# Twelve one-column sums issued between the matmuls of a gate product

## What is computed

```python
def mla_branch(c_q, c_kv, k_rope, q_norm, kv_norm, w_uq, w_ukv, cos, sin):
    q = (rms_norm(c_q, q_norm) @ w_uq).reshape(bsz, seq, A_HEADS, A_NOPE + A_ROPE)
    kv = (rms_norm(c_kv, kv_norm) @ w_ukv).reshape(bsz, seq, A_HEADS, A_NOPE + A_V)
    k_rope = apply_rope(k_rope, cos, sin)
    ...
for layer in range(DEPTH):
    u = rms_norm(h, norm_pre[layer])
    proj = u @ w_in[layer]
    ...
    y_a = mla_branch(a_cq, a_ckv, a_kr, ...) * jax.nn.silu(a_g)
    ...
    y = jnp.concatenate([y_a, y_b, y_c, y_d], axis=-1) @ w_out[layer]
    h = h + rms_norm(y, norm_post[layer])
```

## Time and profile before

| | |
|---|---|
| time, median of 3 runs | 740.94 us (738.87 to 741.82) |
| the profiled execution | 739.99 us, its span 738.1 us |
| busy share of the span | PE 92%, VectorE 59%, ScalarE 45%, GpSimd 33% |
| mean granted clock of TensorE | 0.97 |
| sums of squares, layer 0 / layer 1 | 4.78 / 3.96 us on PE |

### The profile page before, as it was taken

How to read it: one execution, slowest core, us unless ns; L and a number is a source line. 1 busy time by engine, 2 the same in 40 slices (tenths; PEclk the granted TensorE clock), 3 DMA queues, 4 the chain that set the end, 5 groups by cost and what they waited for, 6 DMA issues and landing times. The chain is left out here.

```text
span 738.1 us, 10470 instructions
## 1 busy us (share of the span) xinstructions
PE 677.0 (92%) x3836; PEld 545.8 (74%) x3836; DVE 437.5 (59%) x1067; ACT 328.5 (45%) x750; POOL 242.3 (33%) x208
## 2 busy tenths in 40 slices
PE   3996999999999999789998999999999999978996
PEld 3885977888796674448997888778788777444896
DVE  4211597889886754661182148888978955566114
ACT  4422544656241634771434344456533344577121
POOL 1352352354254631000434344425323544210030
PEclk9998999999999977999999999999999998899999
DMA  8367874423122210303253387742322221030202
GB/s 266 96 221 227 261 221 117 130 72 117 57 72 72 72 57 1 114 1 112 84 143 122 119 257 229 193 128 88 101 72 72 72 73 58 0 115 1 73 29 101
DMA packets 66754, 81.48 MB, mean 110 GB/s; under 512 B 10720, under 2 KB 52320, under 8 KB 66703
## 3 DMA queue, kind: packets, MB, share of 16 engines
q1 hardware_dynamic: 66703, 80.81, 35.5%
HBM read 70.28 MB, written 13.93 MB: 114 GB/s over the span
## 5 line engine op out<-in xcount | busy, mean ns | idle before, releaser
L697 POOL TENSOR_TENSOR w_low<-w_raw,w_high 128x512 fp32r<-128x512 f32 (+2 forms) x156 | 199.9, 1314 | 397.3 <-ACT w_high L737 397.3
L1219 PE MATMUL bank<-uT,w_high 128*128 128x512 f32 x400 | 160.0, 400 | 0.0
L1221 PE MATMUL bank<-uT,w_low 128*128 128x512 f32 x400 | 158.2, 396 | 0.0
L1220 PE MATMUL bank<-uT,w_high 128*128 128x512 f32 x400 | 157.9, 395 | 0.0
L841 ACT ACTIVATE probs<-probs,negmax 128x128 f32<-128x128 f32 (+3 forms) x160 | 88.8, 558 | 89.9 <-DVE negmax L1074 89.6
L1219 PEld LDWEIGHTS bank<-uT,w_high 128*128 128x128 f32 x400 | 75.5, 189 | 18.3 <-issue 1.6
L1221 PEld LDWEIGHTS bank<-uT,w_low 128*128 128x128 f32 x400 | 75.3, 188 | 17.8
L1220 PEld LDWEIGHTS bank<-uT,w_high 128*128 128x128 f32 x400 | 75.6, 189 | 16.3
L737 ACT ACTIVATE w_high<-w_raw 128x2048 fp32r<-128x2048 f32 (+2 forms) x40 | 74.7, 1867 | 28.7 <-DMA w_raw<-in_w_out 23.8
L1219 PE MATMUL bank<-w_high,mix 128*128 128x256 f32 x256 | 72.4, 283 | 1.0 <-DVE mix L1159 1.0
L1221 PE MATMUL bank<-w_high,mix 128*128 128x256 f32 x256 | 71.6, 280 | 0.0
(11 more groups left out here) (145 smaller groups left out, 1091.4 us busy)
## 6 DMA issues: line engine op xcount, KB each, us to landing
w_raw<-in_w_in SPq DMA_DIRECT2D x28, 1024.0 KB, 5.4
w_raw<-in_w_out SPq DMA_DIRECT2D x8, 1024.0 KB, 4.9
parts_dram<-staging SPq DMA_DIRECT2D x12, 512.0 KB, 4.9
strips<-strips_dram SPq DMA_DIRECT2D x24, 256.0 KB, 4.2
dqk<-parts_dram SPq DMA_DIRECT2D x24, 256.0 KB, 4.2
hX<-in_x SPq DMA_DIRECT2D x8, 512.0 KB, 6.0
strips_dram<-table_dram SPq DMA_DIRECT2D x1, 3328.0 KB
qidx<-parts_dram SPq DMA_DIRECT2D x12, 256.0 KB, 4.2
```

Of the source, the lines that this page charges most:

```text
L697: ins = nc.gpsimd.tensor_tensor(w_low[:, s, ks, 0:w], w_raw[:, s, ks, 0:w], w_high[:, s, ks, 0:w].bitcast(F32), ALU.subtract)
L1219: nc.tensor.matmul(out_ap, lh, rh, start=start, stop=False)
L1220: nc.tensor.matmul(out_ap, lh, rl, start=False, stop=False)
L1221: return nc.tensor.matmul(out_ap, ll, rh, start=False, stop=stop)
```

## The change

The twelve sums are no longer a block of their own. `aup_head` moves ahead of the gate product `("unit", "ga", 1)`, and on PE it now only waits for the squares and takes the bank. The product's loop over its eight chunks puts, in each of the first four, one sum behind each of its three matmuls; the last sum counts up `unit_ready`. The transposes of the rotary key and VectorE's work on them become a step of their own, `krturn`, right behind the product. VectorE's folding and means stay with `aup_head` and so come ahead of the gate's evacuation. The units are numbered anew (sums, gate, rotary key in place of gate, sums, rotary key), and one VectorE copy falls away.

```diff
-SQUARES_AT, AUP_HEAD_AT = 8, 9
+SQUARES_AT = 8
+SQUARES_IN = ("unit", "ga", 1)
@@ layer_steps
         for e in ex[:half]:
-            st += [e] + topk(r[1])
+            st += [("aup_head",), e, ("krturn",)] if e == SQUARES_IN else [e] + topk(r[1])
...
-        st += {SQUARES_AT: [("squares_a",)], AUP_HEAD_AT: [("aup_head",)]}.get(j, [])
+        st += [("squares_a",)] if j == SQUARES_AT else []
@@ units_of
-    if k == "aup_head":
-        return ["dve", "dve"]
+    if k in ("aup_head", "krturn"):
+        return ["dve"]
@@ vector
                     nc.vector.tensor_copy(coef[:, 0, 0:1], s8[:, 0:1]).then_inc(emptied_by["dve"], 1)
-                    dve.wait_ge(unit_ready, n + 2)
-                    after(nc.vector.tensor_copy(krx[:], bank[:, unit_bank(n + 1), 0:NB * A_ROPE].rearrange(
-                        "p (t r) -> p t r", t=NB)))
+                if kind == "krturn":
+                    n = l * NU + UNIT_AT[step]
+                    dve.wait_ge(unit_ready, n + 1)
+                    nc.vector.tensor_copy(krx[:], bank[:, unit_bank(n), 0:NB * A_ROPE].rearrange(
+                        "p (t r) -> p t r", t=NB)).then_inc(emptied_by["dve"], 1)
+                    wait_unit_emptied(dve, n)
                     hr = A_ROPE // 2
...
-                    nc.vector.tensor_copy(coef[:, 0, 0:1], krx[:, 0, 0:1]).then_inc(emptied_by["dve"], 1)
@@ tensor
+                        elif step == SQUARES_IN:
+                            cs = slice(c * P, (c + 1) * P)
+                            sb, ts = squares_bank, slice(k * P, (k + 1) * P)
+                            nc.tensor.matmul(b, w_high[:, s, k, cs], uT[:, 0, k, :], start=k == 0, stop=False)
+                            if k < NB:
+                                nc.tensor.matmul(sb[:, k:k + 1], sq[:, 0, ts], ones[:], start=True, stop=False)
+                            nc.tensor.matmul(b, w_high[:, s, k, cs], uT[:, 1, k, :], start=False, stop=False)
+                            if k < NB:
+                                nc.tensor.matmul(sb[:, k:k + 1], sq[0:64, 1, ts], ones[0:64, :], start=False, stop=True)
+                            ins = nc.tensor.matmul(b, w_low[:, s, k, cs], uT[:, 0, k, :], start=False, stop=k == KC - 1)
+                            if k < NB:
+                                last_square = nc.tensor.matmul(sb[:, 4 + k:5 + k], sq[:, 2, ts], ones[:],
+                                                               start=True, stop=True)
+                            if k == NB - 1:
+                                last_square.then_inc(unit_ready, 1)
...
                 if kind == "aup_head":
-                    n = l * NU + UNIT_AT[step]
                     pe.wait_ge(lat_squared, l + 1)
-                    b = work_bank(n)
-                    for tb in range(NB):
-                        ts = slice(tb * P, (tb + 1) * P)
-                        nc.tensor.matmul(b[:, tb:tb + 1], sq[:, 0, ts], ones[:], start=True, stop=False)
-                        nc.tensor.matmul(b[:, tb:tb + 1], sq[0:64, 1, ts], ones[0:64, :], start=False, stop=True)
-                        ins = nc.tensor.matmul(b[:, 4 + tb:5 + tb], sq[:, 2, ts], ones[:], start=True, stop=True)
-                    ins.then_inc(unit_ready, 1)
-                    b = work_bank(n + 1)
+                    squares_bank = work_bank(l * NU + UNIT_AT[step])
+                if kind == "krturn":
+                    b = work_bank(l * NU + UNIT_AT[step])
```

## The result

The changed kernel takes 747.04 us (739.82 to 753.11, 15 executions) against 740.96 us (736.69 to 749.04) for the kernel before in the same comparison: ratio 1.0063, 95% interval 1.0037 to 1.0089. That is slower by 0.6%, and outside the predicted range. By the medians the change costs between 3.7 and 6.1 us, where 0.4 us less was predicted. A ratio leaves out, of every kernel, executions over 1.5% above its fastest (slow ones), while medians and times at half clock are over all its executions.

The account below looks back on a forecast made before the run. TensorE, at half clock after the one-column sums, bounds the kernel. A layer sums 8.7 + 10.1 + 4.9 + 1.5 = 25.2 us, 1.6 less in layer 0, 1.3 more in layer 1: 740.94 - 0.3, rounded to 740.5 us; range 734.0 to 745.0.

Parts of the forecast that it names:

- The sums among the matmuls: Sums between the gate product's large matmuls: next to nothing hidden, 0.27 us each, 3.2 us a layer (1.7 to 5.0).
- The product and the clock: Gate product with its sums: clock stays up, PE done 8.7 us after its start (5.5 plus 3.2).
- Rival 2: Gate product mixed with sums is too thin, clock falls within it: 750 us, one layer 745; chance 0.10.
- What is late next: Ahead of aup 1: PE idles some 3.4 us for VectorE's tokq copy, until 10.1 us behind the product's end.
- The other edits: Folding, rotary key operations, GpSimd's root and one copy less, off PE: free or covered, no time gained or lost.
- The prediction's opening: Three stretches around branch A's sums: TensorE busy throughout at half its clock, VectorE 50 to 75%, ScalarE a quarter.
- The clock in the wait: Ahead of aup 1, both layers: clock falls in or just behind the wait; aup 1 4.9, transposes 1.5 us; chance 0.55.
- rival 1: Clock holds through the wait ahead of aup 1: 734.8 us, one layer about 738; chance 0.17 both layers, 0.10 one.
- I count it at nothing elsewhere.: Outside the stretch from gate product to job 10's scores: no change, since the same code runs before and behind.

Follow-up runs that it names:

- e9_rows128: The kernel of e6_chain with each second sum over 128 rows instead of 64, the upper 64 zeros written by ScalarE; 732.91 us, ratio 0.9869 to the kernel before.
- e2_filled: The changed kernel with three extra, unread pairs of matmuls between aup 0 and aup 1, where PE idled; 736.51 us, ratio 0.9938 to the kernel before.
- e0_after: The changed kernel measured again in a second comparison, no edit; 745.11 us, ratio 1.0049 to the kernel before.
- e1_block: The changed kernel's order of steps, but the twelve sums as one block ahead of the gate product; 754.41 us, ratio 1.0159 to the kernel before.
- e10_convonly: The changed kernel with only the conversion of weight group 17 moved from the gate product to aup 1; 743.86 us, ratio 1.0003 to the kernel before.
- e8_fill1: The changed kernel with one extra pair of matmuls between aup 0 and aup 1; 741.08 us, ratio 0.9977 to the kernel before.
- e4_mixlate: The changed kernel with step mix 6 moved from job 9 to job 10, behind tokq; 744.67 us, ratio 1.0037 to the kernel before.
- e6_chain: The changed kernel with mix 6 moved to job 11 and weight group 17's conversion to aup 1; 734.25 us, ratio 0.9908 to the kernel before.

## Why the prediction was wrong

**The sums among the matmuls.** Right in kind: next to nothing is hidden. The term was mis-sized: a sum costs (6.63 - 12 x 0.237) / 12 = 0.316 us, not 0.27, so 3.8 instead of 3.2 us a layer. A single figure was the mistake: 0.24 us where the sum has 128 rows, 0.48 where it has 64, and in e9_rows128, with 128 rows throughout, 0.22. The ten sums between the two of the earlier trace rows include both forms, and were read as one pace. On the timeline before, a row further down would have told it:

```profile
265.93 0.38 PE L1371 MATMUL bank<-ones,sq 128*128 128x1 f32 x2
266.24 0.38 PE L1372 MATMUL bank<-ones,sq 64*128 64x1 f32 x2
266.55 0.38 PE L1373 MATMUL bank<-ones,sq 128*128 128x1 f32 x2
266.79 0.36 PE L1371 MATMUL bank<-ones,sq 128*128 128x1 f32 x2
```

From 128 rows to 64 and back it is 0.31 us from start to start, between two of 128 rows 0.24 us. So a 64-row sum among 128-row ones is 0.14 us dearer than one of them, which the mean of 0.28 hides; between large matmuls it is 0.24 us dearer. e9_rows128 shows that the row count is what costs; why more so among large matmuls, no run shows.

**The product and the clock.** It held, as forecast. Rival 2 fell. The product with its sums took 9.6 instead of 8.7 us. A slip has part in that: the 5.5 us taken for the large matmuls reach to the last one's start; to the next kind it is 263.65 - 258.00 = 5.65 us.

**What is late next.** Right: a new wait ahead of aup 1, for tokq, in both layers, 3.03 us for 3.4; aup 1 starts 9.75 us behind the product's end (265.12) instead of 10.1. The other edits did not lengthen the chain, as forecast: VectorE's mix starts 5.21 us behind the product's end, before 5.31. The prediction's opening reads VectorE at 50 to 75% and ScalarE at a quarter in all three stretches; by the earlier trace rows VectorE has 23 to 24% in the first, and ScalarE 63 and 76% in the block. Nothing in the sum rests on it.

**The clock in the wait.** It fell in the wait or just behind it in both layers of both traces, where rival 1 had it hold. Up to job 10's scores the sum came out: 50.45 us in the two layers, forecast 2 x 25.2. That is in part luck, since errors cancel in it: the product is 0.9 us longer in each layer, the way from it to aup 1 0.35 us shorter, and in layer 1 aup 1 began at full clock (1.3 us less).

**"I count it at nothing elsewhere."** This is the step that failed. The prediction priced the half clock with aup 1 and seven transposes, 6.4 us a layer, let it end where the measured stretch ended, and put the rest of the kernel at nothing. In the kernel before the clock had fallen inside the block, and was back when job 10's scores came, at 284.6 in layer 0 and 632.8 in layer 1. Now it falls later and can reach over other work: up to 293.8 in the first trace, where scores to aup 2 take 12.12 instead of 7.70 us, and 4.6 us more go between the two layers' stretches. In the second trace neither happens, and that execution's 740.09 us are the forecast's 740.5. So the forecast is the low edge of the changed kernel's times and not their median.

The medians say the same: the forecast meant some 14 us less at half clock than the profile before has (6.4 a layer in place of 17.1 and 10.2), about 30 us; measured are 38 and 48. At 0.37 us each, these 8 to 18 us are 3 to 7 us, which is about what is missing. e2_filled shows the cause by undoing it; the arithmetic of this paragraph is worked out, not shown.

**Rival 1's price** was about right, though the case did not occur: with the clock held (e2_filled), product to scores takes 22.83 us (22.3 forecast), and the kernel 736.51 us (734.8).

**Open.** The first trace's other stretches at half clock, 324.5 to 331.4 and 590.8 to 594.2, stand in neither the trace before nor e0_after's. Both falls lie in waits of 1.95 and 1.71 us that all three traces have, so the waits are not new, and e1_block's trace shows both falls too. Whether the change makes such falls more frequent or they belong to the execution, no run here tells; with it stays open how much of the median loss lies in the two stretches around the product.

## What to carry to other kernels

A stall that is taken from the busy engine under reduced clock can uncover the chain that ran in its shadow: work out at full clock who is late next, and shorten that chain first (here mix and conversion out of the way: 1.0049 to 1.0063 became 0.9908). An idle wait of TensorE is priced with the work behind it at half clock, and that work does not end where the measured stretch ended; bound it by the longest stretch any trace shows, and compare the mean granted clock of many executions before one trace is trusted. If the wait can't be removed, discarded matmuls in it can pay (e2_filled).

## What the runs showed of the hardware

- Behind equal idle waits of 3.03 us in the same code, TensorE stayed at 1.2 GHz for 3.4 us, 6.8 us or 20.5 us, though it was busy 11.36 of 12.12 us in the last case. The time at half clock ran from 25 to 57 us between executions of one kernel, and took the time from 739.8 to 753.1 us with it.
- Shorter waits had falls too: in one of 1.64 us (e10_convonly, layer 1), and 1.8 to 1.9 us behind ones of 2.17 us (e8_fill1, both layers). Behind the 1.63 us wait of e10_convonly's layer 0 the clock stayed up for 7.7 us.
- A one-column sum of 64 rows between matmuls of 128 rows costs twice one of 128 rows (0.48 against 0.24 us), so zeros in the missing rows are cheaper on TensorE than leaving them out: twelve sums with their large matmuls took 5.46 instead of 6.63 us (e9_rows128).
- Beside GpSimd's conversion VectorE's scaling took 3.30 us (e4_mixlate; 1.27 without, e6_chain) and its mix 1.66 us (0.69 without, e10_convonly).
